# A matrix-memory stage unrolled over its heads, with scores and turned keys made once for both scan directions

## The reference

```
def step(carry, inp):                       # one chunk of one head
    c_st, n_st, m_st = carry
    b = lax.cumsum(fc, axis=2)
    d = where(lower, b[t] - b[s] + ic[s], -inf)
    inter = b + m_st
    m_t = maximum(inter, max(d, axis=-1))
    w = exp(d - m_t);  a_inter = exp(inter - m_t)
    s = einsum('bhtd,bhsd->bhts', qc, kc) * w
    num = einsum('bhts,bhsd->bhtd', s, vc) + a_inter * einsum('bhtk,bhkd->bhtd', qc, c_st)
    den = sum(s, axis=-1) + a_inter * einsum('bhtk,bhk->bht', qc, n_st)
    h = num / maximum(abs(den), exp(-m_t))
    kw = kc * w_tok
    c_new = decay * c_st + einsum('bhsk,bhsd->bhkd', kw, vc)
    n_new = decay * n_st + sum(kw, axis=2)
...
for direction in range(2):                  # forward, and over the flipped tokens
    hc, st = mlstm_chunkwise(f(qc), f(kc), f(vc), ..., mlstm_zero_state())
    hl, _  = mlstm_chunkwise(f(ql), f(kl), f(vl), ..., st)
    h_lat += f(hl);  h_ctx += f(hc)
```

## Time and profile before

| what | value |
|---|---|
| median of three runs | 3575.5 us |
| the profiled execution's own time | 3573.71 us |
| its span, from first to last instruction | 3570.5 us |
| PE busy over the span | 3135.9 us (88%) |
| DVE, ACT, POOL busy | 1529.5, 1212.9, 147.8 us |
| mean granted clock of PE | 0.938 of full speed |
| first and last PE start in `stage_even` | 282.32 and some 1614.5 us |

### The profile page before, as it was taken

One profiled execution on the slowest core, in us unless ns is written; L12 is line 12 of the kernel. 1 busy time (PEld: TensorE's weight loads), 2 busy tenths in 40 slices (PEclk: granted clock), 3 DMA queues, 4 the chain that ended last, 5 costly groups with the idle time before them and its releaser, 6 DMA issues. The chain is left out here.

```text
span 3570.5 us, 43051 instructions
## 1 busy us (share of the span) xinstructions
PE 3135.9 (88%) x16797; PEld 2670.6 (75%) x16797; DVE 1529.5 (43%) x2588; ACT 1212.9 (34%) x1951; POOL 147.8 (4%) x146
## 2 busy tenths in 40 slices
PE   4538999999999999995995868789999999999598
PEld 4427898889889988983774646668888888887476
DVE  4352454145325523543232121146656665665333
ACT  2321222223222312322212221146666666665310
POOL 0000000000000000000221000000000000000022
PEclk7768999999999999998997989889999999999899
DMA  5401111111111111115333112100010000000332
GB/s 183 159 1 43 30 35 40 46 32 32 45 36 32 32 51 30 32 32 185 95 100 107 38 44 79 62 25 30 28 31 20 26 28 31 21 28 18 124 118 65
DMA packets 214950, 196.06 MB, mean 55 GB/s; under 512 B 9950, under 2 KB 190574, under 8 KB 214770
## 3 DMA queue, kind: packets, MB, share of 16 engines
q1 hardware_dynamic: 197316, 162.62, 14.8%
q0 software_dynamic: 7056, 25.69, 2.0%
q10 hardware_dynamic: 10400, 5.24, 0.5%
HBM read 152.62 MB, written 40.91 MB: 54 GB/s over the span
## 5 line engine op out<-in xcount | busy, mean ns | idle before, releaser
L40 PE MATMUL v_pj<-e_u_hi,v_w_hi 128*128 128x512 f32 (+1 forms) x1728 | 624.5, 361 | 19.3 <-issue 10.3
L41 PE MATMUL v_pj<-e_u_lo,v_w_hi 128*128 128x512 f32 (+1 forms) x1728 | 620.6, 359 | 0.6 <-issue 0.4
L42 PE MATMUL v_pj<-e_u_hi,v_w_lo 128*128 128x512 f32 (+1 forms) x1728 | 620.4, 359 | 0.0
L40 PEld LDWEIGHTS v_pj<-e_u_hi,v_w_hi 128*128 128x128 f32 x1728 | 329.8, 191 | 67.0 <-issue 20.1
L42 PEld LDWEIGHTS v_pj<-e_u_hi,v_w_lo 128*128 128x128 f32 x1728 | 329.3, 191 | 51.8 <-issue 0.7
L41 PEld LDWEIGHTS v_pj<-e_u_lo,v_w_hi 128*128 128x128 f32 x1728 | 329.9, 191 | 47.1
L40 PE MATMUL o_y_bank<-o_w_hi,o_m_hi 128*128 128x512 f32 x576 | 235.9, 410 | 71.9 <-DVE o_w_lo L1095 69.5
L1592 ACT CAST t_pt_hi<-t_ring 128x512 fp32r<-128x512 f32 (+1 forms) x384 | 181.3, 517 | 252.2 <-PE t_ring L1775 252.2
L40 PE MATMUL l_pj<-l_u_hi,l_w_hi 128*128 128x512 f32 (+3 forms) x376 | 160.8, 428 | 81.8 <-DVE l_w_lo L1323 60.7
L41 PE MATMUL o_y_bank<-o_w_lo,o_m_hi 128*128 128x512 f32 x576 | 231.5, 402 | 0.0
L42 PE MATMUL o_y_bank<-o_w_hi,o_m_lo 128*128 128x512 f32 x576 | 231.0, 401 | 0.0
(11 more groups left out here) (327 smaller groups left out, 6219.6 us busy)
## 6 DMA issues: line engine op xcount, KB each, us to landing
v_w_raw<-in_ev_w_in SPq DMA_DIRECT2D x73, 512.0 KB, 3.8
m_w_raw<-in_mod_w SPq DMA_DIRECT2D x24, 1024.0 KB, 5.7
l_w_raw<-in_od_w_in SPq DMA_DIRECT2D x21, 512.0 KB, 4.0
o_m_raw<-mixT SPq DMA_DIRECT2D x20, 512.0 KB, 3.8
mixT<-v_buf SPq DMA_DIRECT2D x16, 512.0 KB, 2.7
o_w_raw<-in_ev_w_out SPq DMA_DIRECT2D x16, 512.0 KB, 3.4
zgT<-l_lat POOLq DMA_DIRECT2D x16, 512.0 KB, 3.1
t_zg<-zgT SPq DMA_DIRECT2D x32, 256.0 KB, 2.7
```

Of the source, the lines that this page charges most:

```text
L40: nc.tensor.matmul(out, whi, xhi, start=first, stop=False)
L41: nc.tensor.matmul(out, whi, xlo, start=False, stop=False)
L42: return nc.tensor.matmul(out, wlo, xhi, start=False, stop=last)
```

## The change

It has these parts.

- `stage_even` is written out for all four heads; no engine has a loop or a register there, and every wait is for a constant. The list of tiles, steps and counts is made in the program that builds the kernel.
- The key-query products and the turned keys of a chunk, which do not depend on the direction, are made once (`prepare`), ahead of the steps, in tiles 4 and 5. DVE copies them from the bank to `s_all` and `k_tok` (`prepared`). These two lie over `k_lo` and `k_hi`, whose chunk is then no longer needed.
- R goes to DRAM at the end of `stage_gates` as rows, and SP loads it for each step, spread over the 128 partitions, into one of two buffers `wgt[d]`; GpSimd adds the mask; ACT takes the exponential there. The diagonal, the matmul of ones and that of the mask are gone.
- The values have a column of ones already (`v_hi[:, :, 256:258]`); Z now takes 258 columns and has two banks, so that the normaliser comes with it. The two-column matmuls are gone, and DVE updates state and normaliser in one operation.
- `st_done` is split in `y_done`, `z_done` and `x_done`. The convolution's weights are loaded once, ahead of the first split.

The diff, cut to its core:

```diff
+            sp.wait_ge(logf, 6)
+            for d in range(2):
+                sp.dma_start(a["r_rows"][4 * d:4 * d + 4, :], rows2("R")[32 * d:32 * d + 4, :]).then_inc(row_out, 16)
+            sp.wait_ge(row_out, 32)
...
+    PREPARED = {(4, 0): (0, 1), (4, 1): (2, 3), (4, 2): (4, 5), (5, 0): (6, 7), (5, 2): (8, 9)}
...
+            def load_row(h, n, d):
+                c = chunk(n, d)
+                old = step_at[(h, n, d)] - 4
+                if old > 0:
+                    sp.wait_ge(sw_ok, old)
+                row = a["r_rows"][4 * d + h:4 * d + h + 1, c * P:c * P + P]
+                sp.dma_start(wgt[d][n % 2][:, :], row.partition_broadcast(P)).then_inc(rows_in[d][n % 2], 16)
...
+            load_w(0, 0)
             sp.dma_start(buf[0][:, 0:2 * P].rearrange("p (d t) -> p d t", d=2), a["c_mask"].rearrange("d s t -> s d t")).then_inc(const_in, 16)
-            sp.dma_start(w_raw[:, :, :], w_src[:, :, TILES[0][0]:TILES[0][0] + P]).then_inc(raw_in, 16)
+            sp.dma_start(conv_w[:, :, :], a["conv_t"].rearrange("(m p) w -> p m w", p=P)).then_inc(cw_in, 16)
+            for h, t in tiles:
+                if tile_no[(h, t)] + 1 < len(tiles):
+                    load_w(*tiles[tile_no[(h, t)] + 1])
+                n = step_of(t)
+                if n is not None:
+                    nxt = (h, n + 2) if n + 2 < NT else (h + 1, n + 2 - NT)
+                    if nxt[0] < HEADS:
+                        for d in range(2):
+                            load_row(*nxt, d)
...
+        @block.gpsimd
+        def _(pool):
+            pool.wait_ge(const_ok, 1)
+            for h, n, d in steps:
+                x = n % 2
+                pool.wait_ge(rows_in[d][x], 16 * (h * (NT // 2) + n // 2 + 1))
+                pool.tensor_tensor(wgt[d][x][:, :], wgt[d][x][:, :], mask[:, d, :], ALU.add).then_inc(masked, 1)
...
+            def prepared(h, c):
+                dve.wait_ge(prep_done, prep_at[(h, c)])
+                bank = prep_bank(c)
+                nc.vector.tensor_copy(s_all[:, c, :], bank[:, 0:P])
+                nc.vector.tensor_copy(k_tok[:, :, c, :], bank[:, P:3 * P].rearrange("p (j e) -> p j e", e=P)).then_inc(prep_ok, 1)
...
-                nc.vector.tensor_scalar(diag[d][:, :], ident[:, :], hc[:, 1, c, d:d + 1], None, ALU.mult).then_inc(diag_ok, 1)
...
+                    if prev in with_inter:
+                        pe.wait_ge(inter_ok, with_inter[prev])
+                    pe.wait_ge(c_ok, with_state[(h, n - 1, d)])
...
                 if n < NT - 1:
+                    pe.wait_ge(kw_lo_ok, g)
+                    if prev in with_state:
+                        pe.wait_ge(c_f_ok, with_state[prev])
                     for j in range(2):
                         kj = slice(j * P, (j + 1) * P)
-                        mm3(nc, Z[:, j, :], (kw[d][0][:, kj], kw[d][1][:, kj]), (v_hi[:, c, 0:HD], v_lo[:, c, 0:HD]))
-                        nc.tensor.matmul(Y_n[:, j, :], kw[d][0][:, kj], ones_r[:, :], start=True, stop=False)
-                        nc.tensor.matmul(Y_n[:, j, :], kw[d][1][:, kj], ones_r[:, :], start=False, stop=True)
-                pe.wait_ge(sw_ok, i * NSTEP + g + 1)
-                mm3(nc, X, (sw[d][0][:, :], sw[d][1][:, :]), (v_hi[:, c, :], v_lo[:, c, :])).then_inc(st_done, 1)
+                        last = mm3(nc, Z[:, j, :], (kw[d][0][:, kj], kw[d][1][:, kj]), (v_hi[:, c, :], v_lo[:, c, :]))
+                    last.then_inc(z_done, 1)
+                pe.wait_ge(sw_ok, g)
+                if prev:
+                    pe.wait_ge(num_ok, step_at[prev])
+                mm3(nc, X, (sw[d][0][:, :], sw[d][1][:, :]), (v_hi[:, c, :], v_lo[:, c, :])).then_inc(x_done, 1)
...
-            with pe.Fori(0, HEADS) as i:
-                for t in range(NTILE):
-                    n = t - FIRST_STEP_TILE
-                    pe.wait_ge(w_ok, i * NTILE + t + 1)
-                    project(i, t, 0)
-                    if 0 <= n < NT:
-                        scores(i, n, 0)
-                        scores(i, n, 1)
-                    project(i, t, 1)
...
+            for h, t in tiles:
+                n = step_of(t)
+                pe.wait_ge(w_ok, tile_no[(h, t)] + 1)
+                for j in range(3):
+                    project(h, t, j)
+                    for c in PREPARED.get((t, j), ()):
+                        prepare(h, c)
+                    if t in (5, 6) and j == 1:
+                        v_transposes(h, t - 5)
+                    if n is not None and j:
+                        state(h, n, j - 1)
```

More of the change, by code:

```diff
@@ L479, in _, with before @@
+        def before(h, n, d):
+            m = step_at[(h, n, d)] - 1
+            return steps[m - 1] if m else None
         @block.sync
         def _(sp):
-            sp.dma_start(buf[0][:, 0:2 * P].rearrange("p (d t) -> p d t", d=2), a["c_mask"].rearrange("d s t -> s d t")).then_inc(const_in, 16)
-            sp.dma_start(w_raw[:, :, :], w_src[:, :, TILES[0][0]:TILES[0][0] + P]).then_inc(raw_in, 16)
-            def store(i, which, row0, done):
-                rows = mix_rows[bass.ds(i * 2 + row0, 1)]
-                sp.dma_start(rows[:, :, 0:CTX], buf[which][:, 1:1 + CTX]).then_inc(mix_out, 16)
-                sp.dma_start(rows[:, :, CTX:T], buf[which][:, CTX + 3:T + 3]).then_inc(mix_out, 16)
@@ new lines, in _ @@
+            act.wait_ge(const_in, 16)
+            nc.scalar.copy(mask[:, :, :], buf[0][:, 0:2 * P].rearrange("p (d t) -> p d t", d=2))
+            nc.scalar.copy(ident_r[:, :], ident[:, :]).then_inc(const_ok, 1)
+            act.wait_ge(cw_in, 16)
+            split(0, 0)
+            for h, t in tiles:
+                n = step_of(t)
+                if tile_no[(h, t)] + 1 < len(tiles):
+                    split(*tiles[tile_no[(h, t)] + 1])
+                if t in (5, 6):
+                    for g in range(3):
+                        v_hi_part(h, t - 5, g)
+                evacuate(h, t, 0)
+                if n is not None:
+                    weights(h, n, 0)
+                    weights(h, n, 1)
+                    scores_hi(h, n, 0)
+                    scores_hi(h, n, 1)
+                evacuate(h, t, 1)
+                if n is not None:
+                    after_state(h, n, 0)
+                evacuate(h, t, 2)
+                if KIND[t] == "conv_x":
+                    middle_tap(h, t)
+                if n is not None:
+                    after_state(h, n, 1)
@@ L621, in _ @@
                 nc.vector.memset(buf[b][:, :], 0.0)
-            nc.vector.memset(ones[:, :], 1.0)
-            nc.vector.memset(f(ones_r[:, :]), 1.0)
             nc.vector.memset(f(v_hi[:, :, HD:HD + 2]), 1.0)
@@ L846, in scores, with state @@
-                last.then_inc(sc_done, 1)
-            def state(i, n, d):
-                c, g = (n if d == 0 else BWD[n]), 2 * n + d
-                t0 = c * P
+                    nc.tensor.matmul(bank[:, (1 + j) * P:(2 + j) * P], k_hi[:, j, t0:t0 + P], ident_r[:, :], start=True, stop=False)
+                    last = nc.tensor.matmul(bank[:, (1 + j) * P:(2 + j) * P], k_lo[:, j, t0:t0 + P], ident_r[:, :], start=False, stop=True)
+                last.then_inc(prep_done, 1)
+            def state(h, n, d):
+                st = (h, n, d)
+                c, g = chunk(n, d), step_at[st]
+                t0, prev = c * P, before(h, n, d)
@@ L1811, in _, with numbered, over, next_offset @@
                 ring_op(op)
+def numbered(events):
+    return {e: n + 1 for n, e in enumerate(events)}
+def over(nc, name, shape, dt, offset):
+    return nc.alloc_sbuf_tensor_at(name, shape, dt, offset=offset)
+def next_offset(nc):
+    return (nc.sbuf_base + 31) // 32 * 32
 def constants():
```

547 lines of the change are left out of this document (252 added, 295 removed).

## The result

The changed kernel is faster. Beside the kernel before it took 3451.66 us in the median (3447.45 to 3452.65, 4 runs) against 3575.61 us: ratio 0.965, 95% interval 0.9633 to 0.9667, 124.0 us less. It ran twice more as a control among the experiments: 3456.03 against 3575.71 us and 3455.03 against 3573.39 us, 119.7 and 118.4 us less.

The account below looks back on a forecast made before the run. It took the number of PE matmuls and the distance between their starts as the bound. 71.8 + 31.3 + 10.3 + 6.0 - 2.0 - 0.5 = 116.9 us gave 3458 us; range 3452 to 3466, with the first rival 3449 to 3476.

Parts of the forecast that it names:

- scores and turned keys: Tiles 4 and 5 make them once per pair of chunks, 2.23 us, instead of 2.91 us per step: gain 71.8 us.
- normaliser: In `state`, dropping the two-column matmuls saves 0.44 us in each of 72 calls, less 0.4 us for wider matmuls: gain 31.3 us.
- jumps, and clock behind them: At three head borders, PE's "issue" waits go, gain 10.3 us; half-clock work behind them goes, 6.0 us, bounds 0 and 7.3.
- cover lost behind the taps: Behind taps of tiles 7 and 11, PE reaches `state` before DVE's weights: 2 us lost over eight places, bounds 0 and 4.
- start: wait for the first weights: At `stage_even`'s start, splits wait for the convolution's weights in 12-byte pieces: loss 0 to 2 us, taken as 0.5.
- three kinds and no more: PE's waits in the even stage: 10.3 us for "issue", 9.0 us at the start, 3.7 us at the heads' ends.
- What SP queues: Weight loads queued behind broadcast loads still arrive in time; at a head's border with 1.4 us in hand: cost nothing.
- Late weights: Rival: at head borders stores delay tile 1's weights, PE waits as long, 16.3 us given back: 3475 us; chance 8%.
- DVE as bound: Rival: PE waits 0.5 us for DVE in every `state`, 36 us lost: 3494 us; chance 6%.
- short matmuls nearly free: Rival: the normaliser's two-column matmuls cost only 25 ns each, so 24 us less gain: 3482 us; chance 2%.
- the slower case by SP's queue: Rival: broadcast loads hold up weight loads on SP, every step tile stops PE, 4 us each: 3618 us; chance 2%.
- Fetching of the straight code: Rival: PE's fourfold code must be fetched, a 0.4 us stop in each of 72 tiles: 3487 us; chance 3%.

## Why the prediction was right

The stage in the profile gave 120.8 us. The terms, as predicted and as read:

| term | predicted | read |
|---|---|---|
| scores and turned keys | 71.8 | 71.8 (2.23 us a pair); put back, 2.86 a tile of the 2.91 |
| normaliser | 31.3 | 31.5 (30.7 over the 72 `state` calls, and the 0.8 below); put back, 30.7 of the 31.7 |
| jumps, and clock behind them | 10.3 + 6.0 | 18.1 (6.5 + 6.3 + 5.3): waits 10.3, clock 6.1, starting again 0.9, second stops 1.0, which is 0.2 more than read |
| cover lost behind the taps | -2.0 | -0.8 |
| start: clock of the first tile | not there | +0.9 |
| start: wait for the first weights | -0.5 | -1.8 (ahead of the stage's 120.8) |
| not explained | | -0.7 |
| sum | 116.9 | 119.0 |

**Scores and normaliser** came out within 1 us together, by what is left unexplained and by what they cost when put back. Both are distances between starts read in one place and multiplied, in a stage where PE never stops. The rule of 25 ns for a short matmul would have taken 24 us off this; the kernel that put them back decides against it.

**Jumps and clock** are the step that was sized too small, by 1.8 us. Last transposes to the third q piece's copy were 21.19, 21.01 and 20.01 us before and are 14.69 after. The idle part, 10.3, was read. The part at half clock was my estimate, and it was right: by narrow windows PE worked 5.5, 5.7 and 3.0 us at 0.50, 14.2 in all, worth 6.1. What the sum had at nothing is that a stopped PE loses 0.3 us in starting again, 0.9 for three borders, and the second stop behind each jump, 1.0 us in all; the earlier trace rows shows the three long waits alone, and the prediction's "three kinds and no more" passed over that stop. So 7.8 us stood behind the waits, just over my bound of 7.3. Reading the stretch from one fixed event to another, as done here, would have needed no estimate: a border at full clock was computable from 14.1 us of projections.

**The taps.** In tile 8 of the second head Z starts behind Y's last matmul with 0.14 us where 0.12 is usual, is itself drawn to 0.22, and X's first to 0.20:

```profile
721.19 0.28 PE L42 MATMUL v_y<-v_c_st_hi,v_q_lo 128*128 128x258 f32 x1
721.33 0.39 PE L40 MATMUL v_z<-v_vv_hi,v_kw_hi 128*128 128x258 f32 x1
721.55 0.28 PE L41 MATMUL v_z<-v_vv_lo,v_kw_hi 128*128 128x258 f32 x1
...
722.15 0.36 PE L40 MATMUL v_x<-v_vv_hi,v_sw_hi 128*128 128x258 f32 x1
722.35 0.28 PE L41 MATMUL v_x<-v_vv_lo,v_sw_hi 128*128 128x258 f32 x1
```

The whole lasts 2.00 us instead of 1.81: 0.19 us, the lower end of the 0.2 to 0.5 that I had. In tile 12 of that head it is 1.81 (791.45 to 793.26), so nothing is lost behind tile 11, as the prediction's own sentence had it. Four places make 0.8 us. The 2 us of the sum counted eight, against that sentence.

**The start** was mis-sized, and for a reason other than the one named. I had the convolution's 12-byte pieces in view. They landed in time. It was the mask, 128 KB behind 512 KB of weights. DVE's clearing of two buffers, 2.5 us, waits for ACT's casts of mask and identity and stands ahead of the weights' lower half, as shown above:

```profile
271.24 0.57 SPq L527 DMA_DIRECT2D v_buf<-in_c_mask  x1
```

```profile
275.59 0.40 ACT L645 CAST v_mask<-v_buf 128x256 bf16<-128x256 f32 x1 [13.43 <-DMA v_buf<-in_c_mask]
275.90 0.29 ACT L646 CAST v_ident_r<-k_ident 128x128 fp32r<-128x128 f32 x1
276.10 1.04 ACT L565 CAST v_w_hi<-v_w_raw 128x1024 fp32r<-128x1024 f32 x1
```

4.35 us from request to cast; asked first it is 2.25, and then the 12-byte pieces are what comes last, by 0.45 us on DVE. So the reason that I named was the next in line. The loss of 1.8 lies inside the bound of 2, and 0.9 of it came back as clock (3.2 us of work at 0.50 instead of 5.1), which the sum did not have.

**What SP queues** was right in kind and pessimistic in size. At the border the weights were asked for at 587.53 and split by 594.6, against PE's need at 598.4: 3.8 us in hand, where I had 1.4. In an ordinary tile DVE's `sw_lo` is done at 771.0 and X wants it at 775.25, 4.3 us where I had 1.8; before, it still waited for the `scores`, which are gone.

**From 119 to 124.** The first comparison gave 5 us more than the terms, the two controls 119.7 and 118.4. The rest of that profile, behind the stage, was 1954.0 us after, 1956.0 before, and 1957.7 and 1958.0 in the controls: code that the change doesn't touch moves by 4 us from execution to execution, ahead of the stage (280.46, 285.40 and 284.11 to the first projection) as much again. The sum was nearer to the effect than the first result was. Part of that nearness is chance: jumps too small by 1.8 us, taps too large by 1.2, the start too small by 1.3 with 0.9 back.

**The rivals.** Late weights, DVE as bound, short matmuls nearly free and the slower case by SP's queue each left no trace, beyond the 0.8 us behind the taps, and the kernels above that provoke them show where they begin: DVE behind tile 7 at once, behind tile 11 from 0.5 us on and elsewhere not before 1.5, the queue not before one more load a row. Fetching of the straight code: no wait for "issue" in the stage. The Trainium skill says why a sequential run of code is cheap ("Runtime: NRT & Kernel Launch", "Instruction fetch mechanics": it is fetched ahead in order, and a taken jump to a target outside the fetched part stops the engine until that is fetched). The kernel with the loop alone written out agrees, with 10.3 us of such waits before and none after; that a fetch is what they waited for, no run here shows.

## What to carry to other kernels

Where one engine's starts are evenly spaced for a whole stage, an edit is worth its count times the distance between starts, and the distance must take in the matmul behind: a pair of two-column matmuls cost 0.22 us here, nearly two full ones. A loop's jump costs its own wait, the start after it and then the clock behind it, so measure from a fixed event ahead of the border to one past the slow stretch. When a term is smaller than the scatter of whole runs, compare stretches inside the profiles, and run the same kernel twice to see which stretches repeat.

## What the runs showed that I had not expected

- A wait for a semaphore can stand in the profile as "issue" (6.3 us in 3 waits, in the kernel that holds PE for the gating).
- Waits of 2.1 us were followed by 3.4 us at a clock of 0.50 at two borders of three, and left it at 1.00 at the other; waits of 5.8 us brought 6.8 us at 0.50 each time, waits of 0.92 us and of 1.4 us none. A part of the slow stretch that falls on the wait itself costs nothing.
- Starting PE again after a wait cost 0.3 us with the clock at 1.00 throughout.
- Shortening PE's wait at a cold start by 2.15 us gave back 1.2: the stretch at half clock behind it grew by 0.96.
- 80 more broadcast loads of 64 KB raised the weights' landing from 4.7 to 5.6 us and cost no time.
